# Block-sparse decode attention: one 32-column tile of TensorE's array per head, in plain fp32, in place of 16-row accumulations with split values

## What is computed

```python
def moba_sample(q, k, v, k_pool, v_pool, page_table, tab):      # per decode sequence
    k_past = k_pool[page_table]                                 # 8 pages of 128 keys, 4 heads x 128
    means = k_past in blocks of 256, mean over the block
    idx = top 3 of q . means                                    # 3 of the 4 blocks, per token and head
    logits = q . k (selected blocks and own 4 tokens) + relative-position bias
    p = softmax(logits)
    return p[selected] @ v[selected] + p[own] @ v_own
```

## Time and profile before

| | us |
|---|---|
| median of 3 runs (2230.7 to 2231.3) | 2230.83 |
| the profiled execution | 2233.92 |
| its span, first to last instruction | 2232.1 |
| TensorE busy | 2106.2 (94%) |
| VectorE busy | 1114.1 (50%) |
| ScalarE busy | 773.3 (35%) |
| mean granted TensorE clock | 0.966 of full |

### The profile page before, as it was taken

How to read it: one execution, slowest core, us unless ns; L and a number is a source line. 1 busy time by engine, 2 the same in 40 slices (tenths; PEclk the granted TensorE clock), 3 DMA queues, 4 the chain that set the end, 5 groups by cost and what they waited for, 6 DMA issues and landing times.

```text
span 2232.1 us, 37003 instructions
## 1 busy us (share of the span) xinstructions
PE 2106.2 (94%) x14921; PEld 1929.6 (86%) x14921; DVE 1114.1 (50%) x1108; ACT 773.3 (35%) x643; POOL 81.8 (4%) x172
## 2 busy tenths in 40 slices
PE   7999986799988999999998979999999999999995
PEld 5999984344447999999998969999999999999995
DVE  4333335455553444434443365556555655665664
ACT  4333332323334333333332423433333333333332
POOL 0000003000000000000000000100000000000001
PEclk9999996899989999999999989999999999999998
DMA  6545521576764445454456523555666565666541
GB/s 227 168 167 169 183 76 38 154 198 183 198 194 138 158 156 170 155 167 162 159 170 190 168 94 114 170 168 167 217 211 216 203 212 200 216 207 211 202 146 57
DMA packets 190628, 377.01 MB, mean 169 GB/s; under 512 B 9737, under 2 KB 34593, under 8 KB 189002
## 3 DMA queue, kind: packets, MB, share of 16 engines
q1 hardware_dynamic: 184300, 340.50, 47.5%
q10 hardware_dynamic: 6247, 35.31, 4.0%
HBM read 365.43 MB, written 37.66 MB: 181 GB/s over the span
## 4 chain that ended last, share of the span: by engine, by line
PE 91%; DVE 5%; ACT 2%; issue 1%; SPq 0%; ACTq 0%; DMA 0%; DVEq 0%
PE ps L1509 25%; PE ps L1511 25%; PE ps L1510 25%; PE ps L1491 4%; PE ps L1712 3%; PE ps L1497 1%; DVE m_T L1042 1%; PE ps L1815 1%; PE ps L1816 1%; PE ps L1827 1%; PE ps L1824 1%; PE ps L1830 0%; PE ps L1768 0%; PE ps L1660 0%; DVE w_lo L1025 0%
## 5 line engine op out<-in xcount | busy, mean ns | idle before, releaser
L1025 DVE TENSOR_TENSOR w_lo<-w_raw,w_hi 128x2048 fp32r<-128x2048 f32 (+1 forms) x272 | 614.6, 2260 | 786.2 <-ACT w_hi L705 786.2
L1509 PE MATMUL ps<-xn_hi,w_hi 128*128 128x288 f32 x3104 | 916.9, 295 | 27.9 <-DVE xn_lo L1048 13.8
L1511 PE MATMUL ps<-xn_hi,w_lo 128*128 128x288 f32 x3104 | 918.2, 296 | 0.0
L1510 PE MATMUL ps<-xn_lo,w_hi 128*128 128x288 f32 x3104 | 916.3, 295 | 0.0
L705 ACT ACTIVATE w_hi<-w_raw 128x2048 fp32r<-128x2048 f32 (+1 forms) x272 | 514.3, 1892 | 1042.5 <-PE ps L1511 1029.4
L1509 PEld LDWEIGHTS ps<-xn_hi,w_hi 128*128 128x128 f32 x3104 | 584.7, 188 | 32.3 <-DVE xn_lo L1048 15.4
L1510 PEld LDWEIGHTS ps<-xn_lo,w_hi 128*128 128x128 f32 x3104 | 584.6, 188 | 0.0
L1511 PEld LDWEIGHTS ps<-xn_hi,w_lo 128*128 128x128 f32 x3104 | 584.6, 188 | 0.0
L1509 PE MATMUL ps<-act_hi,w_hi 128*128 128x288 f32 x704 | 207.8, 295 | 2.8 <-DVE act_lo L1410 2.8
L1511 PE MATMUL ps<-act_hi,w_lo 128*128 128x288 f32 x704 | 208.5, 296 | 0.0
L1510 PE MATMUL ps<-act_lo,w_hi 128*128 128x288 f32 x704 | 208.0, 295 | 0.0
(11 more groups left out here) (274 smaller groups left out, 1691.3 us busy)
## 6 DMA issues: line engine op xcount, KB each, us to landing
w_raw<-in_w_in SPq DMA_DIRECT2D x104, 1024.0 KB, 5.0
w_raw<-in_w_up SPq DMA_DIRECT2D x88, 1024.0 KB, 5.0
w_raw<-in_w_down SPq DMA_DIRECT2D x44, 1024.0 KB, 5.1
kv<-in_cache_k SPq DMA_DIRECT2D x64, 256.0 KB, 2.9
kv<-in_cache_v SPq DMA_DIRECT2D x64, 256.0 KB, 2.9
w_raw<-in_w_o SPq DMA_DIRECT2D x16, 1024.0 KB, 5.1
out<-in_cache_win ACTq DMA_DIRECT2D x32, 512.0 KB, 4.2
kv<-in_cache_win SPq DMA_DIRECT2D x16, 512.0 KB, 6.4
```

The costliest lines, as they stand in the source:

```text
L1025: e.tensor_tensor(w_lo[s][:, 0:k, 0:n], w_raw[slot][:, 0:k, 0:n], w_hi[s][:, 0:k, 0:n].bitcast(F32), ALU.subtract).then_inc(lo_ready, 1)
L1509: e.matmul(dst, w_hi[s][:, r, cols], x_hi[:, k0 + r, :], start=first and r == 0, stop=False)
L1510: e.matmul(dst, w_hi[s][:, r, cols], x_lo[:, k0 + r, :], start=False, stop=False)
L1511: mm = e.matmul(dst, w_lo[s][:, r, cols], x_hi[:, k0 + r, :], start=False, stop=last and r == k - 1)
```

## The change

Each of the four heads gets 32 columns of the array and the 32 partitions of PSUM that belong to them. `qs_b` becomes [128, 4, 32], zero but for 4 columns per head; the score matmuls of a half are issued together, once all its four key groups are turned and copied, into partitions 32h to 32h+31, without accumulation over heads. `kt_b` grows from two slots to eight (in the room of `v_hi`), and key groups use two PSUM banks by turns in place of three. `L_b`, the bias and the small statistics have 128 partitions (32 per head, 4 of them meaningful). The transposes of `L_b` are 128 wide. The value product takes a head's values (128 columns) with that head's probabilities, in plain fp32 straight from the landed pages: `v_hi`, `v_lo`, `own_hi`, `own_lo` and the split of `pt_b` are gone. The normalisation of `L_b` is gone too; its factor is applied when ScalarE copies the output (`ob`), which is now 128x128. Of the zero-padded `qpad_b` nothing is left: GpSimd copies queries straight out of `z_own`. GpSimd also clears the new `pt_b`, after the prompt's last value product.

```diff
-    kt_b = sb("kt_b", [P, 2, 512], F32, R_SPLIT + 9472)
+    kt_b = sb("kt_b", [P, 2, B_HEADS, 512], F32, R_VTOK)
-    L_b = sb("L_b", [16, PAST + NS], F32, R_SPLIT + 21760)
+    L_b = sb("L_b", [P, PAST + NS], F32, R_SPLIT + 22272)
-    v_hi = [sb(f"v_hi{s}", [P, 4, 512], F32R, R_VTOK + 8192 * s) for s in range(2)]
-    v_lo = [sb(f"v_lo{s}", [P, 4, 512], F32R, R_Z + 8192 * (4 + s)) for s in range(2)]
+    pt_b = sb("pt_b", [P, 9, B_HEADS, 32], F32, R_SPLIT + 9472)
...
-            for half in range(2):
-                e.wait_ge(kv_landed[4 + half], i * 64 + 64)
-                e.activation(v_hi[half][:, :, :], kv[4 + half][:, :, :], ACT.Copy)\
-                    .then_inc(act.sem, act.step(name(("v_hi", half))))
...
-            e.activation(ob[:, :], ps[0:32, 3, :], ACT.Copy)\
+            e.wait_ge(dve.sem, at(dve, "rs_b"))
+            e.activation(ob[:, :], ps[:, 2, 0:P], ACT.Identity, scale=col[:, 2:3])\
...
-            e.tensor_scalar(L_b[:, :], L_b[:, :], col[0:16, 2:3], None, ALU.mult)\
-                .then_inc(dve.sem, dve.step(name("P_b")))
...
-            if q >= 3:
-                e.wait_ge(keys_even if q % 2 else keys_odd, n * 4 + ((q - 3) // 2 + 1))
+            if q >= 2:
+                e.wait_ge(keys_odd if q % 2 else keys_even, n * 4 + q // 2)
...
-        def scores(n, q, at):
-            half, h = q // 4, q % 4
-            e.wait_ge(keys_odd if q % 2 else keys_even, n * 4 + (q // 2 + 1))
-            if q == 0:
+        def scores(n, half, at):
+            e.wait_ge(keys_even, n * 4 + (2 * half + 2))
+            e.wait_ge(keys_odd, n * 4 + (2 * half + 2))
+            if half == 0:
...
-            e.matmul(ps[0:16, 4 + half, :], qs_b[:, 16 * h:16 * h + 16], kt_b[:, q % 2, :],
-                     start=h == 0, stop=h == 3).then_inc(scored, 1)
+            for h in range(B_HEADS):
+                mm = e.matmul(ps[32 * h:32 * h + 32, 4 + half, :], qs_b[:, h, :], kt_b[:, half, h, :],
+                              start=True, stop=True)
+            mm.then_inc(scored, 1)
...
+            need = value(at(act, ("kt_a", 0)))
             e.wait_ge(pool.sem, pool.at("ident"))
             e.wait_ge(win_landed[0][1], i * 16 + 16)
-            e.wait_ge(keys_odd, i * 4 + 4)
+            e.wait_ge(act.sem, need)
...
-                keys(nxt, 2, 6, at)
+                keys(nxt, 2, 5, at)
+                scores(nxt, 0, at)
+                keys(nxt, 5, 6, at)
...
             for pg in range(8):
-                turn(ps[:, 7, 16 * pg:16 * pg + 16], L_b[:, pg * P:pg * P + P], 16)
-            turn(ps[0:NS, 7, 128:144], L_b[:, PAST:PAST + NS], 16).then_inc(pe.sem, pe.step(name("ptb")))
+                if pg == 4:
+                    e.wait_ge(dve.sem, at(dve, "o_a", back=1))
+                turn(ps[:, 7 if pg < 4 else 3, pg % 4 * P:pg % 4 * P + P], L_b[:, pg * P:pg * P + P], P)
+            turn(ps[0:NS, 2, P:2 * P], L_b[:, PAST:PAST + NS], P).then_inc(pe.sem, pe.step(name("ptb")))
...
-                e.matmul(ps[0:32, 3, :], pt_b[0:k, pg, :], hi_v, start=pg == 0, stop=False, skip_group_check=True)
-                mm = e.matmul(ps[0:16, 3, :], pt_b[0:k, pg, 0:16], lo_v, start=False, stop=pg == 8,
-                              skip_group_check=True)
+                for h in range(B_HEADS):
+                    v = kv[4 + pg // 4][:, pg % 4, h * P:h * P + P] if pg < 8 \
+                        else v_own[:, 768 + h * P:768 + h * P + P]
+                    mm = e.matmul(ps[32 * h:32 * h + 32, 2, 0:P], pt_b[0:P if pg < 8 else NS, pg, h, :], v,
+                                  start=pg == 0, stop=pg == 8, skip_group_check=True)
...
-            for h in range(4):
-                mm = turn(ps[:, 7, 32 * h:32 * h + 32], ob[:, h * P:h * P + P], 32)
-            mm.then_inc(pe.sem, pe.step(name("otb")))
+            turn(ps[:, 2, 256:384], ob[:, :], P).then_inc(pe.sem, pe.step(name("otb")))
             if not last:
-                scores(nxt, 7, at)
+                scores(nxt, 1, at)
```

More of the change, by code:

```diff
@@ L125, in constants @@
     return {"c_prompt": prompt.reshape(33, 4 * 384), "c_sample": sample, "c_ramp": ramp,
-            "c_spread": spread, "c_same": same, "c_rank": np.tile(np.arange(1, 5, dtype=np.float32), (16, 1))}
+            "c_spread": spread, "c_same": same, "c_rank": np.tile(np.arange(1, 5, dtype=np.float32), (P, 1))}
 S_PAST, S_W0 = 0, PAST + 3
@@ L246, in build @@
     stat = keep("stat", [P, 3, TOK])
-    hist_rows = sb("hist_rows", [120, 512], F32, small[0])
-    qpad_b = keep("qpad_b", [P, NB, 64])
+    hist_rows = keep("hist_rows", [120, 512])
     v_own = keep("v_own", [NS, 1280])
-    pt_b = keep("pt_b", [P, 9, 32], F32R)
     z_own = keep("z_own", [P, 30, NS])
@@ L269, in build @@
     win0 = keep("win0", [P, 512])
[L270 removed]
+    qs_b = keep("qs_b", [P, B_HEADS, 32])
     qs_a = keep("qs_a", [P, QA])
@@ L602, in _ @@
         e.memset(tab_t[:, :, :, :], 0.0).then_inc(pool.sem, pool.step("tab_t0"))
+        e.memset(tab_b[:, :, :], 0.0).then_inc(pool.sem, pool.step("tab_b0"))
         e.wait_ge(lo_ready, U_MIX)
@@ L635, in _ @@
         e.wait_ge(pool.sem, pool.at("oh_r"))
-        e.memset(qpad_b[:, :, :], 0.0).then_inc(pool.sem, pool.step("qb0"))
+        e.memset(qs_b[:, :, :], 0.0).then_inc(pool.sem, pool.step("qb0"))
         e.memset(qpad_a[:, :, :], 0.0).then_inc(pool.sem, pool.step("qa0"))
         e.memset(pt_a[:, :], 0.0).then_inc(pool.sem, pool.step("pt_a0"))
[L639 to L643, removed]
+        e.wait_ge(pe.sem, pe.at(("PV", NU - 1)))
+        e.memset(pt_b[:, :, :, :], 0.0).then_inc(pool.sem, pool.step("pt_b0"))
+        e.wait_ge(pool.sem, pool.at("pt_b0"))
         for g in range(3):
@@ L1244, in sample @@
             e.wait_ge(pe.sem, at(pe, "own_b"))
[L1245 to L1246 removed]
+            e.scalar_tensor_tensor(out=L_b[:, PAST:PAST + NS], in0=ps[:, 7, 0:NS], scalar=SCALE,
+                                   in1=view(bias_b, P, i * NS + PAST, [[1, NS]]), op0=ALU.mult, op1=ALU.add)\
                 .then_inc(dve.sem, dve.step(name("L_b")))
@@ L1678, in biased, with biased_b @@
             return mm
+        def biased_b(dst, off, n, step):
+            for t in range(NT):
+                mm = e.matmul(dst, tabr_b[:, t, :], oh_r[:, off + step * t:off + step * t + n],
+                              start=t == 0, stop=t == NT - 1)
+            return mm
         for k in range(2):
-            biased(ps[0:16, k, :], A_HEADS, 4, S_PAST + 3 + 512 * k, 512, -1).then_inc(pe.sem, pe.step(("bias_b", k)))
+            biased_b(ps[:, k, :], S_PAST + 3 + 512 * k, 512, -1).then_inc(pe.sem, pe.step(("bias_b", k)))
         biased(ps[0:8, 2, 0:128], 0, 2, S_W0 + 3, 128, -1)
```

166 lines of the change are left out of this document (73 added, 93 removed).

## The result

The changed kernel takes 2178.95 us (median of 4 runs, 2175.82 to 2181.11), against 2230.76 us for the kernel before in the same comparison: a ratio of 0.977, 95% interval 0.976 to 0.978. That is 52 us less where 14 were forecast. The time lies within the range, in its outer part, and 3 us from the value of the first rival, full overlap (2176).

The account below looks back on a forecast made before the run. TensorE's own order of work and its waits bound the kernel. Seven sequences -1.4, start -1.8, first sequence -8.5 and last -2.5 sum to -14.2 us, giving 2217 us; own range 2206 to 2227, with rivals 2172 to 2262.

Parts of the forecast that it names:

- the first rival: Score batches and value product: all four tiles run side by side, passes included; -5.5 us a sequence more, about 2176; chance 0.2.
- All three signs of being wrong: Inner sequence over 1 us off 29.9, first sequence still waiting for a transfer, or time outside 2206 to 2227 us.
- the size of a tiled batch and of the tiled value product: Four-head scores and value product: one of two passes hidden per head, so 2.27 us a batch and 5.1 a product.
- the lower bounds: All four heads side by side: 0.95 us for a batch of scores, 2.2 us for the value product.
- the waits of an inner sequence: TensorE waits for copies in an inner sequence: about 0.4, 1.1, 0.5 and 1.1 us.
- the way to the window scores: Inner sequence, from first window transpose to window scores: 5.2 us in place of 5.10, so +0.1.
- split and normalising: Dropped value split (1.9 us twice, 2.27 twice) and normalising of L_b (0.76): worth nothing in an inner sequence.
- Start: Keys and scores of sequence 0: eight groups until about 422, two batches until 426.7 against 428.5, so -1.8 us.
- First sequence: First decode sequence: without the split nobody waits for value pages and values arrive in time; 38.4 us falls by 8.5.
- Last sequence: Last decode sequence: waits for normalised L_b and pt_b's second half go (0.76 + 1.4), some low clock too; -2.5, between 0 and -5.
- the third rival: Loop clock: added waits bring a low-clock stretch to each sequence, 1.7 us a sequence, +12, about 2229; chance 0.1.

Follow-up runs that it names:

- The one-tile run: Changed kernel with each batch of four score matmuls run once more beforehand, the added four all on tile 0: 2228.6 us.
- the two versions on the split: Changed kernel with the value split's copies put back as load: 2186.6 us; kernel before with unsplit plain fp32 values on the whole array: 2253.5 us.
- the four versions with a longer batch or product: Changed kernel with the value product one head at a time (2225.0 us) or on two tiles (2188.3), or scores doubled on one tile (2228.6) or four (2187.6).
- the version without the waits for copies: Changed kernel with window groups three and four turned in other PSUM banks and two VectorE copies moved earlier: 2175.9 us.
- the last version: Changed kernel without TensorE's four copy waits, window loads on ScalarE's queue, those of the windows' values issued after `oa`: 2166.5 us.

## Why the prediction was wrong

All three signs of being wrong that the prediction named came: an inner sequence 5.6 us off 29.9, a transfer waited for in the first sequence, and a time outside 2206 to 2227.

**Failed: the size of a tiled batch and of the tiled value product**, 2.27 and 5.1 us, "from the order of the passes". They measured 0.99 and 2.23, which are the lower bounds (0.95 and 2.2) that the text had worked out. The premise "every record of TensorE here starts in program order" held for the trace of before, which has no two column tiles at work, and was stretched to a case that it did not contain. The one-tile run shows a start out of order. Two batches and a product make 1.28 x 2 + 2.87 = 5.4 us a sequence, all of what an inner sequence was off (29.7 forecast, 24.3 measured); six times that is 33 us, where forecast and result are 38 apart, and the start and the last sequence had their share of the same error (3.9 and 3.1 us beyond their forecasts). In the traces the difference is 42: to these come 6 us of clock that the forecast did not count on, less 1.3 in the first sequence and 2.0 of later start. The first rival had the mechanism right and its price a sequence (-5.5). Its terms, -38 and -5, make 2173.6 and not the 2176 that stands there, so the nearness to 2179 is a little flattered; its chance of 0.2 was too low against 0.5 for a value that no row supported.

**Right: the waits of an inner sequence**, all four, within 0.25 us each, and the way to the window scores. The forecast said that split and normalising lie beside TensorE's work in an inner sequence; the copies put back cost 0.8 us there, behind a product that had become short.

**Start**: -5.7 for -1.8. Turning the eight groups took 7.1 us (415.75 to 422.81) where 8.2 were put, and the two batches 1.94 us (to 424.75) where 4.7 were put: mostly the same mis-sized batch.

**First sequence**: -7.2 for -8.5. That the dropped split would free it is borne out by the two versions on the split, above (8.3 us without it before, 5.1 for it after). One statement was wrong: it still waits for a transfer, and behind the wait TensorE works at half clock. The wait, and the stretch (columns as in the earlier trace rows):

```profile
446.21 1.02 PE L1804 MATMUL ps<-win,pt_a 128*8 128x256 f32 x2 [4.02 <-DMA win<-in_cache_win]
```

```profile
445.00:451.90 6.90, 5.69 (x14) 1.65 (x15) 0.00 (x0) 0.00 (x0) 0.00 (x0) 0.51 1.07 282
```

The first sequence takes 31.1 us where an undisturbed one takes 24.3: 4.0 of the 6.8 are the wait and 2.8 the clock.

The forecast asked whether the value pages would be there, and not for the windows' values, whose issue stands behind them on SyncE. With the product at 5.1 us, as forecast, most of this wait would have been hidden. The wait also absorbs what is added ahead of it: in the four versions with a longer batch or product the window product comes at 444.7 to 451.8, with no wait for the windows and no half clock behind it, so they lost 5 to 8 us less than their added length times eight.

**Last sequence**: -5.6 for -2.5. The chain behind the exponential shortened as said (a wait of 3.20 us for 4.33 and 1.36), and the product was short again; the low-clock stretch inside it fell from 10.3 us to 3.4 (612.3 to 615.7, clock 0.50).

```profile
611.82 1.74 PE L1468 MATMUL ps<-ident,L_b 128*128 128x128 f32 x9 [3.20 <-ACT L_b L845]
```

**The clock** went against the third rival: the new waits brought no low stretch to each sequence. In these traces six inner sequences lost 0.9 us by it after, some 7 before; in the changed kernel's second trace one lost 1.5. Whether the change itself spared the rest is not shown.

## What to carry to other kernels

Small fp32 products on 32-column tiles gained nearly the full factor here when neighbours in the program sat on different tiles: put the tile in the innermost loop, since the same 36 matmuls took 2.2 us so and 8.8 in the other order. When an unknown lies between two bounds and no row bears on the middle, give the ends their chances rather than a constructed middle value. And where a stage is sped up by a fifth, look at the queue that issues its loads: here two limits, copies and issue, stood level at 24.3 and 24.5 us; lifting one gave 3 us or none, lifting both 12.

## What was not expected of the hardware

- Four passes on four tiles start between 540.15 and 540.175, where 0.03 for each was put from the issue of narrow loads. The 72 passes of 128 columns in 2.23 us are 0.031 each, which looks like that issue floor; it is the streaming of four at a time, 0.124 a group.
- TensorE starts a matmul on a free tile ahead of an earlier one whose tile is taken, and then the earlier pass starts 0.43 us later (491.22, 491.65). The semaphore that the scores raise stands on a batch's last matmul alone; whether an end can come out of order was not tried.
- An issue of a page of 256 KB takes SyncE about 1.06 us (8 in 8.46). In the version without the waits for copies the issues set the period: the transfers moved 247 GB/s over 470 to 600 there, and with six of the 22 issues on another queue the same bytes went in 22.5 us a sequence, at up to 293 GB/s in a stretch of the last version.
- The wait of 4.0 us for a transfer in the first sequence cost more than itself: behind it the granted clock was 0.51, and eight passes of window values took 3.62 us in place of 1.89 (447.02 and 473.67 in the changed kernel's trace).
